# RWKV scan: the substitution of the 16 x 16 diagonal blocks from VectorE to GpSimd, with two buffers for its tiles

## What is computed

```
def step(S, inp):
    r_t, w_t, k_t, v_t, kk_t, b_t = inp
    sa = jnp.einsum('bhij,bhj->bhi', S, -kk_t)
    S = (S * w_t[:, :, None, :] + sa[..., None] * b_t[:, :, None, :]
         + v_t[..., None] * k_t[:, :, None, :])
    return S, jnp.einsum('bhij,bhj->bhi', S, r_t)
```

## Time and profile before

| | us |
|---|---|
| median of 3 runs | 3494.68 |
| lowest, highest | 3493.44, 3499.32 |
| the profiled execution | 3487.46 |
| its span | 3486.2 |
| TensorE busy in the span | 3188.2 (91%) |
| VectorE busy | 2211.3 (63%) |
| GpSimd busy | 469.5 (13%) |

### The profile page before, as it was taken

How to read it: one execution, slowest core, us unless ns; L and a number is a source line. 1 busy time by engine, 2 the same in 40 slices (tenths; PEclk the granted TensorE clock), 3 DMA queues, 4 the chain that set the end, 5 groups by cost and what they waited for, 6 DMA issues and landing times.

```text
span 3486.2 us, 58522 instructions
## 1 busy us (share of the span) xinstructions
PE 3188.2 (91%) x25755; PEld 2622.4 (75%) x25755; DVE 2211.3 (63%) x2948; ACT 971.9 (28%) x1514; POOL 469.5 (13%) x373
## 2 busy tenths in 40 slices
PE   6988788979987999999999897998998799999996
PEld 4777767778885878888888676875667688888885
DVE  5758655778887444444444575997556566666666
ACT  4544233312113221111111444112663111111112
POOL 2530023423224000000000121000001011111110
PEclk9979788989998999999999998999999899999999
DMA  4410044322224011111111202114001111111111
GB/s 131 122 66 14 16 142 138 111 45 42 37 36 166 19 55 51 40 55 53 38 55 43 91 31 74 49 43 99 2 2 61 43 49 49 49 49 49 49 49 67
DMA packets 242726, 207.27 MB, mean 59 GB/s; under 512 B 66744, under 2 KB 205255, under 8 KB 241959
## 3 DMA queue, kind: packets, MB, share of 16 engines
q1 hardware_dynamic: 223527, 176.82, 17.1%
q10 hardware_dynamic: 13824, 25.17, 2.2%
q0 software_dynamic: 5120, 1.53, 0.5%
HBM read 171.93 MB, written 29.64 MB: 58 GB/s over the span
## 4 chain that ended last, share of the span: by engine, by line
PE 70%; DVE 17%; ACT 5%; POOL 2%; issue 2%; DMA 2%; SPq 1%; ACTq 0%; DVEq 0%; POOLq 0%
PE ps L2169 23%; PE ps L2184 17%; PE ps L2031 5%; PE ps L636 3%; PE ps L637 3%; PE ps L638 3%; DVE Yc L2794 2%; DVE s_tmp L1662 2%; DVE s_Z L1663 2%; PE ps L2893 2%; PE ps L2921 1%; PE ps L2911 1%; PE ps L1480 1%; POOL a_x L2544 1%; PE ps L1008 1%
## 5 line engine op out<-in xcount | busy, mean ns | idle before, releaser
L3198 DVE TENSOR_TENSOR H<-H,ps 128x1024 f32<-128x1024 f32 x256 | 312.7, 1221 | 181.6 <-PE ps L2184 174.8
L2334 DVE TENSOR_TENSOR fsum<-fsum,ps 128x1024 f32<-128x1024 f32 x168 | 205.2, 1221 | 312.4 <-PE ps L2184 310.3
L2184 PE MATMUL ps<-dh,hh 128*128 128x512 f32 x864 | 340.0, 393 | 19.9 <-DVE hl L2149 13.9
L2184 PE MATMUL ps<-dl,hh 128*128 128x512 f32 x864 | 338.7, 392 | 0.0
L2184 PE MATMUL ps<-dh,hl 128*128 128x512 f32 x864 | 338.6, 392 | 0.0
L2169 PE MATMUL ps<-hn_h,uh 128*128 128x512 f32 x704 | 275.8, 392 | 7.2 <-DVE ul L1779 4.7
L2169 PE MATMUL ps<-hn_l,uh 128*128 128x512 f32 x704 | 275.4, 391 | 0.0
L2169 PE MATMUL ps<-hn_h,ul 128*128 128x512 f32 x704 | 275.3, 391 | 0.0
L2169 PE MATMUL ps<-hx_h,uh 128*128 128x512 f32 x512 | 200.9, 392 | 8.4 <-DVE hx_l L2149 5.3
L2184 PEld LDWEIGHTS ps<-dh,hh 128*128 128x128 f32 x864 | 163.8, 190 | 58.0 <-DVE hl L2149 15.6
L2169 PE MATMUL ps<-hx_l,uh 128*128 128x512 f32 x512 | 200.4, 391 | 0.0
(11 more groups left out here) (473 smaller groups left out, 7345.8 us busy)
## 6 DMA issues: line engine op xcount, KB each, us to landing
aw<-in_w_ada_dram ACTq DMA_DIRECT2D x96, 256.0 KB, 2.9
uw<-in_w_mlp_dram SPq DMA_DIRECT2D x32, 512.0 KB, 4.3
dw<-in_w_mlp_dram SPq DMA_DIRECT2D x32, 512.0 KB, 5.2
uw<-in_ffn_gate_dram SPq DMA_DIRECT2D x22, 512.0 KB, 4.0
uw<-in_ffn_up_dram SPq DMA_DIRECT2D x22, 512.0 KB, 5.3
dw<-in_ffn_down_dram SPq DMA_DIRECT2D x22, 512.0 KB, 5.9
cw<-in_w_in_dram SPq DMA_DIRECT2D x20, 512.0 KB, 3.8
o_w<-in_w_out_dram SPq DMA_DIRECT2D x16, 512.0 KB, 9.9
```

The lines of the kernel that those rows point to most:

```text
L2184: mm = pe.e.matmul(ps[:, 2 * pair + hf, :], v[s][:, blk(t)], w[:, half(hf)], start=(m == 0), stop=(m == 2))
L2334: return dve.c.tensor_tensor(f, f, new, ALU.add) if g else dve.c.tensor_copy(f, new)
L3198: return dve.c.tensor_tensor(h, h, self.ps[:, 4 + 2 * (t % 2):6 + 2 * (t % 2), :], ALU.add)
```

## The change

The substitution leaves VectorE's program and becomes `substitute_pool` in GpSimd's, with the same 30 operations and the same transposing copy. `N16`, `Z16` and their unit source get 64 partitions, that is two buffers of 32 partitions each, used by even and odd substeps; `tmp16` likewise.

The scratch `nd` gets a layout in which a matrix of 64 x 64 lies in one piece, 64 elements further to the next, so that the four diagonal blocks of both heads of a pair are 8 pieces at one stride. `blocks_there` is then 8 DMAs of 8 partitions instead of 16 of 4, all issued by SP. Its store becomes two DMAs, one for each half of the partitions.

SP's order for substep n becomes: wait for `x16` of n-1 and store zd of n-1, nd stores of n, four loads into ZZ of n-1, eight loads into N16 of n, sig. GpSimd's order becomes: unit fill for n, wait for the loads of N16, substitution of n, wait for the zd store of n, its four loads into ZZ of n. `inverse_back` gets one more wait, for `p4` of n-1, and the SP part of it a counter of its own (`t_zi`).

```diff
-                         ("nd", (2, LANES, PART, CH)), ("zd", (2, 8, 4, 2, 2, 16, 16)), ...
+                         ("nd", (2, LANES, 2, CH * CH + CH)), ("zd", (2, 8, 4, 2, 2, 16, 16)), ...
...
-    def blocks_there(self, eng, counter, n, ks):
-        nd = self.dram["nd"]
-        for k in ks:
+    def blocks_there(self, eng, counter, n, xs):
+        nd = self.dram["nd"][n % 2]
+        for x in xs:
             for d in range(2):
-                eng.e.dma_start(self.N16[4 * k:4 * k + 4, d], nd[n % 2, 4 * d:4 * d + 4, 16 * k:16 * k + 16, 16 * (k % 4):16 * (k % 4) + 16]) \
+                eng.e.dma_start(self.N16[n % 2][8 * x:8 * x + 8, d], bass.AP(tensor=nd.tensor, offset=nd[4 * d + x].offset, ap=[[16 * CH + 16, 8], [CH, 16], [1, 16]])) \
                     .then_inc(*counter.one("in", n))
...
         if n >= 2:
             eng.wait_ge(self.pe["l4", n - 2, 1], self.dve["zz", n - 2, 1])
+        if n:
+            eng.wait_ge(self.pe["p4", n - 1, 0])
...
+        def store(n):
+            sp.wait_ge(self.pool["x16", n])
+            sp.e.dma_start(zd[n % 2].rearrange("k x d w i c -> x k (d w i c)"), self.Z16[n % 2].rearrange("p d w i c -> p (d w i c)")) \
+                .then_inc(*self.t_z.one("out", n))
+
+        def back(n):
+            sp.wait_ge(self.t_z["out", n])
+            self.inverse_back(sp, self.t_zi, n, range(0, 8, 2))
+
         sig(1)
         for n in range(NSUB):
+            if n:
+                store(n - 1)
             sp.wait_ge(dve["nm", n, 1])
-            sp.e.dma_start(nd[n % 2].rearrange("l p c -> p l c"), self.NM[n % 3][:, :, 0, :]).then_inc(*self.t_n.one("out", n))
+            for H in range(2):
+                sp.e.dma_start(nd[n % 2, :, H, 0:CH * CH].rearrange("l (p c) -> p l c", c=CH), self.NM[n % 3][H01[H], :, 0, :]).then_inc(*self.t_n.one("out", n))
             if n:
-                sp.wait_ge(self.t_z["out", n - 1], self.pool["zero"])
-                self.inverse_back(sp, self.t_z, n - 1, range(0, 8, 2))
+                back(n - 1)
             sp.wait_ge(self.t_n["out", n])
-            self.blocks_there(sp, self.t_n, n, range(0, 5))
+            self.blocks_there(sp, self.t_nb, n, range(0, 4))
             if n % 2 and (n + 3) // 2 < NBLK:
                 sig((n + 3) // 2)
-            sp.wait_ge(dve["x16", n])
-            sp.e.dma_start(zd[n % 2].rearrange("k x d w i c -> (k x) (d w i c)"), self.Z16[:].rearrange("p d w i c -> p (d w i c)")) \
-                .then_inc(*self.t_z.one("out", n))
...
     def rwkv_scan_pool(self):
...
+        for n in range(NSUB):
+            if n >= 2:
+                pool.wait_ge(self.t_z["out", n - 2])
+            pool.c.tensor_copy(self.Z16[n % 2][:, :, 1], self.eye16[32 * (n % 2):32 * (n % 2) + 32]).then_inc(*pool.one("one", n))
+            self.substitute_pool(n)
+            pool.wait_ge(self.t_z["out", n], pool["zero"])
+            self.inverse_back(pool, self.t_zb, n, range(1, 8, 2))
...
+    def substitute_pool(self, n):
+        pool, at = self.pool, 32 * (n % 2)
+        pool.wait_ge(self.t_nb["in", n])
...
+        for s in range(15):
...
+            pool.c.tensor_tensor(part, col, pivot, ALU.mult).then_inc(*pool.one())
+            pool.c.tensor_tensor(rows, rows, part, ALU.subtract).then_inc(*pool.one())
+        pool.c.tensor_copy(self.Z16[n % 2][:, :, 0], self.Z16[n % 2][:, :, 1].rearrange("p d i c -> p d c i")).then_inc(*pool.one("x16", n))
```

More of the change, by code:

```diff
@@ L88, in constants @@
     c["lev_mask"] = np.tile(lm.reshape(CH, -1), (2, 1))
-    c["eye16"] = np.tile(np.eye(16, dtype=f).reshape(1, 1, 256), (32, 2, 1)).reshape(32, 512)
+    c["eye16"] = np.tile(np.eye(16, dtype=f).reshape(1, 1, 256), (64, 2, 1)).reshape(64, 512)
     c["stack_eye"] = np.tile(np.eye(CH, dtype=f), (2, 1))
@@ L402, in plan_block1 @@
         self.En, self.Eb = sb("s_En", [PART, LANES, 2, CH]), sb("s_Eb", [PART, LANES, 2, CH + 1])
-        self.eye16, self.N16 = sb("eye16", [32, 2, 16, 16]), sb("s_N16", [32, 2, 16, 16])
+        self.eye16, N16 = sb("eye16", [64, 2, 16, 16]), sb("s_N16", [64, 2, 16, 16])
+        self.N16 = [N16[32 * k:32 * k + 32] for k in range(2)]
         self.XT, self.S = ([sb(n, [PART, LANES, CH]) for k in range(2)] for n in ("s_XT", "s_S"))
         self.T, self.Rn, self.U = (sb(n, [PART, LANES, CH]) for n in ("s_T", "s_Rn", "s_U"))
-        self.tmp16 = put(150, "s_tmp16", [32, 128])
+        self.tmp16 = put(150, "s_tmp16", [64, 128])
         self.room = self.r0 + 150 * 1024 + 800
@@ L412, in plan_block1 @@
         self.room = self.r0 + 184 * 1024
-        self.BKT, self.ZZ2, self.Z16 = [sb("s_BKT", [PART, LANES, 2, CH]) for k in range(3)], sb("s_ZZ2", [PART, LANES, 2, CH]), sb("s_Z16", [32, 2, 2, 16, 16])
+        self.BKT, self.ZZ2, Z16 = [sb("s_BKT", [PART, LANES, 2, CH]) for k in range(3)], sb("s_ZZ2", [PART, LANES, 2, CH]), sb("s_Z16", [64, 2, 2, 16, 16])
+        self.Z16 = [Z16[32 * k:32 * k + 32] for k in range(2)]
         self.room = self.r0 + 16 * 1024
@@ L1441, in sig @@
             sp.e.dma_start(self.sig[:], sg[:, t].rearrange("d p c -> p d c")).then_inc(*self.t_in.one("sig", t))
+        def store(n):
[5 more added lines that the diff above has]
+            self.inverse_back(sp, self.t_zi, n, range(0, 8, 2))
         sig(1)
         for n in range(NSUB):
+            if n:
+                store(n - 1)
             sp.wait_ge(dve["nm", n, 1])
-            sp.e.dma_start(nd[n % 2].rearrange("l p c -> p l c"), self.NM[n % 3][:, :, 0, :]).then_inc(*self.t_n.one("out", n))
+            for H in range(2):
+                sp.e.dma_start(nd[n % 2, :, H, 0:CH * CH].rearrange("l (p c) -> p l c", c=CH), self.NM[n % 3][H01[H], :, 0, :]).then_inc(*self.t_n.one("out", n))
             if n:
-                sp.wait_ge(self.t_z["out", n - 1], self.pool["zero"])
-                self.inverse_back(sp, self.t_z, n - 1, range(0, 8, 2))
+                back(n - 1)
             sp.wait_ge(self.t_n["out", n])
-            self.blocks_there(sp, self.t_n, n, range(0, 5))
+            self.blocks_there(sp, self.t_nb, n, range(0, 4))
             if n % 2 and (n + 3) // 2 < NBLK:
                 sig((n + 3) // 2)
-            sp.wait_ge(dve["x16", n])
-            sp.e.dma_start(zd[n % 2].rearrange("k x d w i c -> (k x) (d w i c)"), self.Z16[:].rearrange("p d w i c -> p (d w i c)")) \
-                .then_inc(*self.t_z.one("out", n))
-        sp.wait_ge(self.t_z["out", NSUB - 1])
-        self.inverse_back(sp, self.t_z, NSUB - 1, range(0, 8, 2))
+        store(NSUB - 1)
+        back(NSUB - 1)
         i = self.i
@@ L1564, in rwkv_scan_pe @@
                 NM_m, ZZ, ZZ2 = self.NM[m % 3], self.ZZ[m % 2], self.ZZ2
-                pe.wait_ge(self.t_z["in", m], self.t_zb["in", m])
+                pe.wait_ge(self.t_zi["in", m], self.t_zb["in", m])
                 for d in range(2):
@@ L1631, in rwkv_scan_pool @@
         pool.e.memset(self.S[0][:], 0.0).then_inc(*pool.one("zero"))
[L1632 to L1640, removed]
-        self.meet(self.pool, "rwkv_scan")
[L1643 to L1650, removed]
+        pool.wait_ge(self.t_misc["r_const"])
+        for n in range(NSUB):
[5 more added lines that the diff above has]
+            self.inverse_back(pool, self.t_zb, n, range(1, 8, 2))
+        self.meet(self.pool, "rwkv_scan")
+    def substitute_pool(self, n):
+        pool, at = self.pool, 32 * (n % 2)
+        pool.wait_ge(self.t_nb["in", n])
+        N, Z = self.N16[n % 2][:, 0], self.Z16[n % 2][:, 0, 1]
         def both(x, second, first, rest):
             return bass.AP(tensor=x.tensor, offset=x.offset + first, ap=[x.ap[0], [second - first, 2]] + rest)
-        for s in range(first, end):
+        for s in range(15):
             p, q, k = 15 - s, s, 15 - s
             zn, nn = 512, 256
-            part = self.tmp16[:, 0:2 * k * (s + 1)].rearrange("p (d i c) -> p d i c", d=2, i=k)
+            part = self.tmp16[at:at + 32, 0:2 * k * (s + 1)].rearrange("p (d i c) -> p d i c", d=2, i=k)
             rows = both(Z, zn + (q + 1) * 16, p, [[16, k], [1, s + 1]])
```

8 lines of the change are left out of this document (2 added, 6 removed).

## The result

The changed kernel takes 3533.88 us (median of four runs, 3523.51 to 3540.55) against 3497.0 us for the kernel before on the same chip: ratio 1.0109, 95% interval 1.0092 to 1.0126, 37 us slower. Forecast were 3566 us, 71 us slower.

What follows compares the result with a forecast made beforehand. VectorE and TensorE were both taken as near the limit, VectorE's serial work ending last. D 9.5 + P 17.3 = 26.8 us against 22.42, +66 over 15 periods, +5 for substep 0: +71, 3566 us; range 3500 to 3660.

Steps and rivals of the forecast that it cites:

- D: Time from the end of one substep's x16 until the next substep's N16 loads have landed: 9.5 us (8.9 to 11).
- P: Time on GpSimd from loads landed to x16, substitution, copy and disturbance together: 17.3 us.
- Rival 1: GpSimd is quick on small shapes: P 10.9 us, TensorE bounds at 20.8 us a period, 3471 us; chance 0.10.
- rival 2: GpSimd is slower than the sum, by short-row patterns or disturbance: P 22.6 us, period 32.1, 3653 us; chance 0.17.
- rival 3: The two buffers do hide the loads: 22.4 us a period on GpSimd, about 3500 us; chance 0.04.
- the forecast's 3505 to 3625: Bounds of the main case, D in series with P and P between 14.5 and 20 us; chance 0.64.
- The gap of the chain of six: Gap between dependent GpSimd operations, from six in a row: 0.145 us, added to each of the 30 substitution operations.
- The disturbance by VectorE: VectorE's products slowing GpSimd's substitution: 1.5 us a period (0 to 4); 3.4 us if all were met as full blocks.
- Substep 0: Start of the scan: SP's loads take 1.6 us less, the substitution 6.9 us more, +5 us.
- nm: VectorE's nm, ready about 22.5 us after an x16, within the period, so the nd stores cost nothing.
- The clock: TensorE's granted clock, likely to fall at times as it idles more; priced at nothing given some 4 us of slack.
- The end: Stretch after the last x16, as before because the DMAs are the same: no cost.

Runs made afterwards that it cites:

- a5: The changed kernel with the N16 loads as 16 DMAs of 4 partitions instead of 8 of 8, all by SP: 3578.31 us.
- a3: The changed kernel with five of the 15 substitution steps left out (wrong inverse): 3479.75 us.
- a2: The changed kernel with one buffer instead of two for N16, Z16 and tmp16: 3535.01 us.
- b2_decoupled: The changed kernel with GpSimd storing zd, SP loading N16 before its ZZ loads, ScalarE issuing the other four ZZ loads, and nm ahead of S: 3518.0 us.
- a1: The changed kernel with N16 and Z16 partitions in the old order, so the zd store is 32 rows at one stride and loads write every fourth partition: 3568.13 us.
- a4: The changed kernel with the substitution put back on VectorE in its old places, all else as changed: 3517.68 us.
- b5: b2_decoupled with SP's four ZZ loads moved to GpSimd, ScalarE's four ahead of the exponentials, and nm behind S as in the changed kernel: 3526.9 us.
- d2: The changed kernel with 48 unused small matmuls a substep in TensorE's idle time before its wait for ZZ: 3533.13 us.
- d1: The changed kernel with 128 unused small matmuls a substep on TensorE before its wait for ZZ: 3569.78 us.

## Why the prediction was right, point by point

- The direction and the mechanism were right. Loads and substitution lie in series because SP issues the loads behind its wait for `x16`; the timelines show D + P = 24.1 us, a5 lengthens D by eight issues and the period by the same 2.9 us, and a3 shortens P until TensorE's side takes over. Rival 1 (GpSimd quick enough for TensorE to bound) fell, rival 2 fell, rival 3 was refuted by a2. The sizes were wrong: a loss of 37 us instead of 71. The period is 24.3 us instead of 26.8, which makes 15 x 2.5 = 38 us too much; the 6.3 us at the end, which I had put at nothing, take some of that back. P even lies below the 14.5 us with which I had bounded the forecast; without the dearer zd store (some 21 us) and the end (6), neither of which I had seen, the time would stand at 3507 us, at the lower edge of the forecast's 3505 to 3625. That it lies well inside is luck.
- The step that was mis-sized most is P: 14.0 us instead of 17.3. (a) The 30 operations take 12.9 us instead of 15.5. From start to start an operation on 30 elements takes 0.31 to 0.33 us, on 128 elements 0.50 to 0.52: about 1.8 ns an element and 0.27 us fixed, against 2.11 ns and 0.33 us in the sum. The gap of the chain of six did not carry over: it is 0.07 to 0.08 us here, not 0.145. The mean of 0.43 us from start to start is just above the 0.4 that the prediction had named as a sign of its being wrong. (b) The transposing copy takes 1.05 us, against 0.62 and a gap. The plain copy takes 0.60. By the estimate from the figures of the Trainium skill (GPSIMD Engine Reference, section 7, Performance pitfalls for Q7 kernels), 2.9 cycles an element for a strided reading instead of 1.9, the strided copy takes 0.4 us more than the plain one. The measured difference is 0.45, so the rule agrees here and the sum should have had it. (c) The disturbance by VectorE, 1.5 us, did not come in the periods but the last. It exists, as substep 0 shows, GpSimd and VectorE in the changed kernel:

```profile
732.54 0.41 POOL L1671 TENSOR_TENSOR s_tmp<-s_N,s_Z 32x120 f32<-32x120 f32 x1
...
733.03 0.83 POOL L1672 TENSOR_TENSOR s_Z<-s_Z,s_tmp 32x120 f32<-32x120 f32 x1
733.51 0.91 DVE L1707 TENSOR_TENSOR s_BK<-r_bb,s_En 128x512 f32<-128x512 f32 x1
```

  Beside the products the operation takes twice as long, the product 0.91 instead of 0.68. The substitution of substep 0 takes 15.3 us, 1.3 more than in the periods and less than the 3.4 us that the prediction names for a full block. But in the periods nm and what follows it end so late (nm at 912.2, `x16` at 912.6) that the products run in D, while GpSimd is waiting. Where the order lets them meet, as in b2_decoupled (P of 15.2 us), the price of 1.5 us is about right. I had the price right and the place wrong.
- D is 10.15 us in the mean instead of 9.5, by two errors that partly cancel: the zd store lands after 3.5 us instead of 2.1, because its shape is new, and the last load lands after 1.7 us (in the period shown) instead of 2.5. I had taken the store's time from the earlier trace rows without noticing that its destination is no longer one stride. The store's own time in a1 puts this at 1.5 us a period, some 22 of the 37 us, and a4 agrees with it (20 us without the substitution's move), with the reservation about the nd stores made there.
- Substep 0 was forecast at +5 and is +4.3, which is luck too: its substitution was put at 15.8 us without disturbance, where it takes 14.0 undisturbed and 15.3 as it ran, and its loads gained 2.6 us (4.1 from the first issue to the first operation), not 1.6. The issues that I put at nothing (nd stores within the wait, GpSimd's issues and fill within D, the wait for p4) were hidden, as the timelines show.
- nm: forecast at 22.5 us after `x16`, with 4 us of slack. It is 23.6 in the period shown (888.55 to 912.17) and 21.8 to 24.2 over the periods, and it ends 0.2 to 2.8 us before the next `x16`, once 0.5 us after it but still ahead of its own nd store. It held, but barely; a3 and b5 show that nm is the next bound.
- The clock: forecast to fall at times and to cost nothing in the periods. Both right, by d2. TensorE was expected to be busy three quarters of the time and is 84%.
- The end was put at nothing and costs 6.3 us. The chain of waits there, changed kernel:

```profile
1108.11 3.38 DMA zd_dram<-s_Z
1111.49 1.81 issue
1113.29 1.70 POOL s_ZZ L1436 x3
1115.00 4.99 DMA s_ZZ<-zd_dram
...
1120.12 1.98 PE ps L1492 x32
```

  From the copy's end to p4 are 12.0 us (1108.11 to 1120.12) instead of 6.3 in the kernel before (1062.43, the end of the last of the earlier trace rows, to 1068.7). 1.5 of the 5.7 us are the store's shape. Another 1.5 are GpSimd's later start: it begins 1.8 us after SP's first load, and not 0.3 us after it as before. The same 1.8 us stand in the other runs in which SP stores zd in the changed kernel's order (a1 to a5, d1, d2); their cause is open. The last 2.8 lie between GpSimd's first issue and p4. Its loads take 5.0 us to land, and SP has issued the load of v, 2 MB, at 1115.24, right behind them in time. That this load is the cause is argued from its place; no run was made for it, but the traces agree. Where v is issued 2 us after GpSimd's first load (changed kernel, a1 to a5, d2), p4 starts 6.3 to 6.8 us after that load; where it is issued 3.5 us (before) or 3.8 us (d1) after it, p4 starts after 4.1 and 5.2 us.

## What to carry to other kernels

A second buffer can hide a load only if nothing that waits for the first buffer's work stands ahead of that load on the issuing queue, and only if the load's own input is there in time, as nm was not in b2_decoupled; read the queue's program order first, then the sizes. A serial chain moved off a busy engine is not off the path when it hangs in a loop with its own loads and stores: the period becomes the loop, and each DMA issue in it counts in full. And when a layout changes, price both ends of every DMA anew, the store as well as the load that it was changed for.

## What the runs showed of the hardware

- The time SyncE's queue takes to issue a small DMA doubled with its shape: a median of 0.32 us for a load of eight neighbouring partitions (0.36 with the gap to the next), 0.66 for one of every fourth (a1); 0.32 for a store of 32 rows at one stride, 0.66 for 4 x 8 rows, which also lands 1.5 us later from the store's start.
- GpSimd, f32 with two inputs on 32 partitions, each waiting for the one before: 0.31 to 0.33 us start to start at 30 elements, 0.50 to 0.52 at 128. VectorE was busy 0.19 us with the first of these, and 0.24 with one in the mean; the 30 operations took 8.3 us there and take 12.9 us here, a ratio of 1.6.
- A GpSimd operation beside VectorE's product of two SBUF tiles took twice its time (0.83 us instead of 0.41 on 120 elements, 0.59 instead of 0.25 on 30), and the product 0.91 us instead of 0.68.
- TensorE, idle for 4.1 us (892.10 to 896.19), came back at a granted clock of 0.56 for p4 and l4 (5.1 us instead of 3.4), and stood at 0.98 over the scan when 2.8 us of the idle time were filled (d2).
